# Layer-norm sums: VectorE adds the eight feature tiles, one tensor product sums over the partitions

## The reference

```python
def layer_norm(x, g, b):
    xf = x.astype(jnp.float32)
    mu = jnp.mean(xf, -1, keepdims=True)
    var = jnp.mean(jnp.square(xf - mu), -1, keepdims=True)
    return ((xf - mu) * lax.rsqrt(var + LN_EPS) * g + b).astype(x.dtype)

h = x * (1 + mod[:, 1]) + mod[:, 0]
x = layer_norm(ALPHA * x + 0.5 * mod[:, 2] * swiglu(h, ...), ln_g[l, 0], ln_b[l, 0])
h = x * (1 + mod[:, 4]) + mod[:, 3]
out, k_a, v_a, k_b, v_b = mixer(l, h)          # one input projection, attention, one output projection
x = layer_norm(ALPHA * x + mod[:, 5] * out, ln_g[l, 1], ln_b[l, 1])
h = x * (1 + mod[:, 7]) + mod[:, 6]
x = layer_norm(ALPHA * x + 0.5 * mod[:, 8] * swiglu(h, ...), ln_g[l, 2], ln_b[l, 2])
```

## Time and profile before

| | us |
|---|---|
| median of 3 runs | 2637.7 |
| lowest and highest run | 2637.45, 2644.15 |
| span of the profiled execution | 2637.8 |
| TensorE busy | 2413.0 (91%) |
| VectorE busy | 894.8 (34%) |
| the two kinds of sums (L504), busy: of `Y`, of `SQ` | 43.0, 53.4 |

### The profile page before, as it was taken

One profiled execution on the slowest core, in us unless ns is written; L12 is line 12 of the kernel. 1 busy time (PEld: TensorE's weight loads), 2 busy tenths in 40 slices (PEclk: granted clock), 3 DMA queues, 4 the chain that ended last, 5 costly groups with the idle time before them and its releaser, 6 DMA issues. The chain is left out here.

```text
span 2637.8 us, 37358 instructions
## 1 busy us (share of the span) xinstructions
PE 2413.0 (91%) x14418; PEld 2238.3 (85%) x14418; DVE 894.8 (34%) x2053; ACT 539.3 (20%) x781; POOL 810.4 (31%) x536
## 2 busy tenths in 40 slices
PE   7899999999999969995898677796999999999996
PEld 4799999999999959983587666785999999999995
DVE  0422221122222390006266766138322222222225
ACT  2211111111111121211133223213111111111114
POOL 2522222322233142223365433433333233222310
PEclk9899999999999989995899888897999999999998
DMA  9532323123111001116810000120111111111101
GB/s 307 185 96 80 95 80 95 55 73 95 32 48 40 17 8 48 48 56 174 203 38 30 17 25 17 35 71 14 48 48 48 48 43 43 41 48 48 40 1 64
DMA packets 211414, 171.56 MB, mean 65 GB/s; under 512 B 31848, under 2 KB 191704, under 8 KB 210841
## 3 DMA queue, kind: packets, MB, share of 16 engines
q1 hardware_dynamic: 211352, 170.76, 21.7%
HBM read 157.24 MB, written 19.26 MB: 67 GB/s over the span
## 5 line engine op out<-in xcount | busy, mean ns | idle before, releaser
L193 PE MATMUL psum<-Hhi,Whi 128*128 128x344 f32 x2736 | 880.9, 322 | 46.0 <-POOL Hlo L660 26.4
L195 PE MATMUL psum<-Hhi,Wlo 128*128 128x344 f32 x2736 | 877.9, 321 | 0.0
L194 PE MATMUL psum<-Hlo,Whi 128*128 128x344 f32 x2736 | 877.5, 321 | 0.0
L289 POOL TENSOR_TENSOR Wlo<-RAW,Whi 128x1024 fp32r<-128x1024 f32 x158 | 381.8, 2435 | 688.1 <-ACT Whi L285 687.4
L193 PEld LDWEIGHTS psum<-Hhi,Whi 128*128 128x128 f32 x2736 | 518.4, 189 | 49.9 <-issue 36.1
L195 PEld LDWEIGHTS psum<-Hhi,Wlo 128*128 128x128 f32 x2736 | 518.2, 189 | 0.0
L194 PEld LDWEIGHTS psum<-Hlo,Whi 128*128 128x128 f32 x2736 | 517.6, 189 | 0.2
L376 DVE TENSOR_TENSOR GF<-SIL,psum 128x344 f32<-128x344 f32 x132 | 67.7, 513 | 897.8 <-ACT SIL L358 897.8
L389 DVE SCALAR_TENSOR_TENSOR Y<-psum,G,Y 128x344 f32<-128x344 f32 (+1 forms) x528 | 302.6, 573 | 181.0 <-PE psum L195 181.0
L193 PE MATMUL psum<-Ghi,Whi 128*128 128x344 f32 x1056 | 339.8, 322 | 1.7 <-DVE yS L392 1.7
L194 PE MATMUL psum<-Glo,Whi 128*128 128x344 f32 x1056 | 338.2, 320 | 0.0
(11 more groups left out here) (196 smaller groups left out, 1889.4 us busy)
## 6 DMA issues: line engine op xcount, KB each, us to landing
ADA<-in_w_ada SPq DMA_DIRECT2D x36, 1024.0 KB, 8.5
RAW<-in_ffn_wg SPq DMA_DIRECT2D x44, 512.0 KB, 3.8
RAW<-in_ffn_wu SPq DMA_DIRECT2D x44, 512.0 KB, 3.8
RAW<-in_ffn_wd SPq DMA_DIRECT2D x44, 512.0 KB, 3.3
RAW<-in_w_in SPq DMA_DIRECT2D x18, 512.0 KB, 3.8
bias_rows<-bias_heads SPq DMA_DIRECT2D x4, 1536.0 KB, 15.8
SK<-in_cache_a_k SPq DMA_DIRECT2D x24, 256.0 KB, 3.3
SK<-in_cache_a_v SPq DMA_DIRECT2D x24, 256.0 KB, 4.2
```

The source lines that it names most:

```text
L193: pe.matmul(out, whi, xhi, start=first, stop=False)
L194: pe.matmul(out, whi, xlo, start=False, stop=False)
L195: return pe.matmul(out, wlo, xhi, start=False, stop=last)
L289: pool.tensor_tensor(Wlo[slot][:, :, :], RAW[raw][:, :, :], Whi[slot][:, :, :].bitcast(F32), ALU.subtract).then_inc(W[phase].ready, 1)
```

## The change

`mean_sum` and `var_sum` are new: one VectorE instruction each, a `tensor_reduce` over the view `p k t -> p t k`, adds the eight feature tiles of a group into the new tile `RED[g]` (128 x 344). `mean_pe` and `var_pe` then wait for that and do a single product of `meanw` with `RED[g]`. The order of all three engines is changed with it. New semaphores are `ln_msum` and `ln_vsum`.

```diff
@@ ffn_pe
                 if norm is not None and g:
-
-                    pe.wait_ge(x.y_evac, UNIT_D * (CH - 1) + KT * g + 3)
                     mean_pe(pe, norm, g - 1)
@@ ffn_dve
+                if norm is not None and g < NG - 1:
+                    dve.wait_ge(x.y_evac, UNIT_D * (CH - 1) + KT * (g + 1) + 3)
+                    mean_sum(dve, norm, g)
                 if norm is not None and g == 1:
                     center(dve, norm, 0)
@@
-        def sum_pe(pe, out, src):
-
-            for k in range(KT):
-                last = pe.matmul(out, meanw[:, :], src(k), start=(k == 0), stop=(k == KT - 1))
-            return last
+        def mean_sum(dve, n, g):
+
+            dve.tensor_reduce(RED[g][:, :], Y[:, :, group(g)].rearrange("p k t -> p t k"), AXX,
+                              ALU.add).then_inc(ln_msum, 1)
+
+        def var_sum(dve, n, g):
+            dve.wait_ge(ln_squared, n.n_at(g))
+            dve.tensor_reduce(RED[g][:, :], SQ[:, :, group(g)].rearrange("p k t -> p t k"), AXX,
+                              ALU.add).then_inc(ln_vsum, 1)
 
         def mean_pe(pe, n, g):
-            sum_pe(pe, bank[MEAN_BANK[g]][:, 0:TG], lambda k: Y[:, k, group(g)]).then_inc(ln_mean, 1)
+            pe.wait_ge(ln_msum, n.n_at(g))
+            pe.matmul(bank[MEAN_BANK[g]][:, 0:TG], meanw[:, :], RED[g][:, :], start=True, stop=True).then_inc(ln_mean, 1)
 
         def var_pe(pe, n, g):
-            pe.wait_ge(ln_squared, n.n_at(g))
-            sum_pe(pe, bank[VAR_BANK[g]][:, 0:TG], lambda k: SQ[:, k, group(g)]).then_inc(ln_var, 1)
+            pe.wait_ge(ln_vsum, n.n_at(g))
+            pe.matmul(bank[VAR_BANK[g]][:, 0:TG], meanw[:, :], RED[g][:, :], start=True, stop=True).then_inc(ln_var, 1)
@@ norm_pe
-            var_pe(pe, n, 0)
             mean_pe(pe, n, 2)
-            var_pe(pe, n, 1)
-            var_pe(pe, n, 2)
+            for g in range(NG):
+                var_pe(pe, n, g)
@@ norm_dve
             center(dve, n, 1)
+            var_sum(dve, n, 0)
+            center(dve, n, 2)
+            var_sum(dve, n, 1)
             scaled(dve, n, 0)
-            center(dve, n, 2)
+            var_sum(dve, n, 2)
             scaled(dve, n, 1)
@@ norm_act
             square(act, n, 0)
             square(act, n, 1)
             std(act, n, 0)
-            if n.i == 1:
-                std(act, n, 1)
+            square(act, n, 2)
+            std(act, n, 1)
             input_hi(act, n, 0, 0)
             input_hi(act, n, 0, 1)
-            square(act, n, 2)
-            if n.i != 1:
-                std(act, n, 1)
@@ vector engine, norm 1 (norm 3 likewise)
             samples_in(dve)
             dve.sem_inc(resid_done, 1)
+            mean_sum(dve, ln[1], 2)
             prep(dve, 3, 4, 0)
@@ vector engine, norm 2
             dve.wait_ge(wout_evac, NG * KT + 6)
+            mean_sum(dve, ln[2], 0)
+            mean_sum(dve, ln[2], 1)
             samples_in(dve)
             dve.sem_inc(resid_done, 1)
+            mean_sum(dve, ln[2], 2)
             prep(dve, 6, 7, 1)
```

More of the change, by code:

```diff
@@ L174, in build @@
             RSTD.append(arena.at(f"RSTD{g}", [P, TG], F32, o)); o += up32(4 * TG)
+        RED = []
+        for g in range(NG):
+            RED.append(arena.at(f"RED{g}", [P, TG], F32, o)); o += up32(4 * TG)
         SQ = arena.at("SQ", [P, KT, T], F32, HOFF + 4 * KT * T)
@@ L249, in build @@
         ln_lo, ln_y, ln_small = (sem(x) for x in ("ln_lo", "ln_y", "ln_small"))
+        ln_msum, ln_vsum = sem("ln_msum"), sem("ln_vsum")
         resid_done = sem("resid_done")
@@ L1830, in _ @@
             dve.sem_inc(resid_done, 1)
+            mean_sum(dve, ln[3], 2)
             prep(dve, None, None, 2, last_norm=True)
```

## The result

| | before | after |
|---|---|---|
| median, us | 2638.0 | 2688.7 |
| lowest and highest run | 2637.45, 2644.15 | 2685.52, 2695.99 |
| span of the profiled execution | 2637.8 | 2686.1 |
| TensorE busy | 2413.0 | 2353.4 |
| VectorE busy | 894.8 | 977.6 |

The ratio is 1.019, with a 95% interval of 1.0176 to 1.0205: the changed kernel is slower. The direction was forecast, with 2672 us; the time lies 17 us above that and just above the range, which ended at 2686.

What follows compares the result with a forecast made beforehand. VectorE's chain was taken to bound the norms, though TensorE, 91% busy, mostly sets the end. Last chunks 6.2, clock 5.0, norms 10.4, 6.4 and 5.9 sum to 33.9 us on 2637.8: 2672 us, range 2646 to 2686.

Steps and rivals of the forecast that it cites:

- R: Time of each of 18 added VectorE reductions: taken as 4.3 us, with 3.0 and 4.9 for the range.
- 24-value row: Profile row of a VectorE reduction of 24 jumping values, 180 ns; gave 1.5 ns a value and R = 4.3 us.
- TensorE's 1.7 ns: TensorE's price a column with jumping operands, from eight records of 256 columns in 3.81 us; gave R = 4.9 us.
- costlier jumps: Rival: banks or the long 4128-byte step put R above 4.9, say 5.9 us; 2684 to 2700 us, chance 0.10.
- Last chunks: Last down-product chunks before norms 1 and 3: TensorE waits for evacuations behind reductions, +3.1 us each, +6.2 together.
- clock: Last chunks: after 5.2 us of TensorE idling, the five last units run at half clock for a while; 2.5 us twice, +5.0.
- norm 1: Four reductions on VectorE less 6.8 us of idling filled, no wait left: 4R - 6.8 = +10.4 us.
- norm 3: Four reductions less 10.4 us of idling, +6.8 us; about 0.9 comes back from ScalarE's earlier last root: +5.9.
- norm 2, to the first subtraction: Three reductions ahead of `prep`, which escapes GpSimd's splits: center 0 at 1782.7 in place of 1778.9, +3.8 us.
- norm 2, behind it: Rest of norm 2: three reductions less 10.3 us of VectorE idling filled, 3R - 10.3 = +2.6 us.
- R + 1.3 - 2.8 and R + 4.3 - 8.3: Last chunk: TensorE's wait at group 1's fourth unit, 2.8 us, and added delay to group 2's fourth unit, +0.3.
- 15 us for each us of R: Whole kernel: added time per us of R, 4 in the last chunks and 4, 3 and 4 in the norms.

Runs made afterwards that it cites:

- e7: Changed kernel with 20 and 34 extra unread TensorE products in the two stalls of each last chunk; 2678.3 us, ratio 1.016.
- e9: Changed kernel with norm 2's `samples_in` moved ahead of its reductions of groups 0 and 1; 2685.2 us against 2689.6 for the changed kernel rerun.
- e4: Changed kernel with only the means summed by reductions, the variance sums again eight products each, new order kept; 2659.1 us, ratio 1.0084.
- e1: Changed kernel with each reduction adding eight neighbouring tokens instead of one token's eight tiles, same counts; 2646.6 us, ratio 1.0035.
- e6: Changed kernel plus 13 VectorE reductions and copies at various steps behind the last output copy; 2752 values took 5.04 us at the real step, 3.02 side by side.

## Why the prediction was wrong in size, point by point

**R, the step that failed.** The term that was mis-sized is R, the time of one reduction: 4.3 us in the sum, 5.1 measured (5.06 to 5.34), eighteen times over. The prediction took 1.5 ns a value from the 24-value row: (180 - 144)/24, with a fixed part of 141 to 144 ns. Measured, the rate is 1.79. Only 24 x 1.79 = 43 ns of that row's 180 are rate; with a fixed part of 137 instead of 141 ns it gives 1.79 as well. An error of 4 ns in the fixed part, divided by 24 and multiplied by 2752, is 0.5 us in R. I named the row nearest in kind and moved its fixed part up only, where moving it down gave 5.1 us. The far larger rows were closer: TensorE's 1.7 ns gave 4.9, the upper bound, still 0.2 short of the measured 5.1. Read more closely that row would have given 5.0: its eight records take 0.63 us each and overlap, so they start (3.81 - 0.63)/7 = 0.45 us apart, 1.77 ns a column. The rival "costlier jumps", which held the time that came (2684 to 2700), had its mechanism wrong: the long step adds next to nothing to one of 16 bytes.

**The formulas with the measured R.** Last chunks 2 x 5.0, clock 5.0, norm 1 4 x 5.08 - 6.8 = 13.5, norm 2 5.9 + 4.9 = 10.8, norm 3 9.0: 48.3 us, which is the measured difference of the spans. That it fits to the tenth is luck, as the terms show:

| us | predicted | with the measured R | measured |
|---|---|---|---|
| last chunks, without the clock | 6.2 | 10.0 | 10.3 |
| clock there | 5.0 | 5.0 | 5.0 |
| norm 1 | 10.4 | 13.5 | 12.6 |
| norm 2, to the first subtraction | 3.8 | 5.9 | 9.2 |
| norm 2, behind it | 2.6 | 4.9 | 5.1 |
| norm 3 | 5.9 | 9.0 | 8.6 |
| everything else | 0 | 0 | -2.5 |

The measured parts of the last chunks come from e7: its chunks, at full clock, are 5.7 and 5.6 us longer than before, less 0.5 each for their longer reductions; the clock is what is left of +8.4 and +6.9.

**Last chunks: right.** They were forecast by R + 1.3 - 2.8 and R + 4.3 - 8.3. With 5.24 and 5.34 these make 3.7 and 1.3 us, 5.0 a chunk; the first stall was 3.59. With the 5.5 and 5.59 of e7 they make 4.0 + 1.6 = 5.6, as its chunks have it.

**Clock: right in size, incomplete in place.** It cost 3.2 and 1.8 us, where 2.5 and 2.5 were forecast. It was not foreseen that the clock also falls at the first stall (0.50 from 898), which it did in chunk 1 and not in chunk 2, at equal stalls of 3.59 us. In e9 the same remainder is 5 us in both chunks and in the second of e4 5.4, so 0 to 3.0 a chunk was too narrow a bound. The cost goes with the time at half clock, which the mean clock of a window gives: 0.88 over 29 us is some 7 us and cost 1.8, 0.83 over 30 us is 10 and cost 3.2, 0.79 over 32 us is 13 and cost 5.

**Norm 1: right in mechanism.** No wait is left but one of 0.62 us for the third root. It came 0.9 below the formula, which is mostly scaled 1: 5.00 us before, beside GpSimd, and 3.99 after, since it now falls into a gap of GpSimd's.

**Norm 2: one thing missed.** The prediction asked how `prep` and the reductions stand to GpSimd's splits and was right on both: the reductions kept their time, and `prep`, pushed behind the splits, ran its eight steps in 1.8 us. It gave `samples_in` 0.5 us in the same stretch, though its first operation has two operands in SBUF, and that cost 4.4 us, as e9 shows. Less the 1.2 that `prep` beat its allowance by, 5.9 becomes 9.1. The recorded sum has a slip of 0.2 us here: 12.9 + 0.5 + 3 from 1766.1 is 1782.5, not 1782.7, and the same sum at R = 4.9 gives 9.8 and not the 9.2 of the range's upper bound. Neither changes the outcome.

**Norm 3: right.** 9.0 by the formula, 8.6 measured.

**The slope.** 15 us for each us of R was too flat. In the formulas themselves it is 4 + 4 + 3 + 3 + 4 = 18; I counted norm 2 once, since GpSimd held `prep` at R = 3.0, though above that both its parts grow. Between e1 and the changed kernel the stretches give some 17.

## What to carry to other kernels

Before work is moved from a busy engine to an idle one, ask who waits for whom in that stretch: TensorE was 91% busy in the whole program and yet not the bound in the norms, where seven eighths of its sums had cost nearly nothing, while VectorE's chain set the end. Cost a strided operation by the step of its innermost reads, with a row that is large enough for the rate to outweigh the fixed part; a row of 24 values can't price one of 2752. And look beside each operation that is pushed later at what GpSimd does by then, and whether rows show that kind of operation waiting for it: here additions of two SBUF operands and one-operand TENSOR_SCALARs did, reductions and the subtraction with an operand in PSUM did not.

## What the runs showed of the hardware

- VectorE's reduction costs 1.05 ns a value at steps of 4 and 8 bytes, 1.32 at 12 and 1.7 to 1.8 from 16 bytes to 4128 (e6, with 0.14 us taken as fixed). A copy of 2752 values goes from 1.59 to 2.65 us when its reads jump and to 3.48 when its writes do: the copy pays in another proportion, and more for writes.
- The reductions of the last chunks took 5.24 and 5.34 us where two of the same shape took 5.06, and 5.50 to 5.59 when TensorE was busy beside them all the time. Why is open.
- A two-operand operation of VectorE of 0.23 us waited 4.4 us for GpSimd and, in three traces, was not let in between two of its instructions; in e4 it was, and so were the steps of `prep` in the kernel before, which each waited for one (2.3 us).
- The price of equal stalls of TensorE (3.59 and 6.11 us) at the clock was 1.8 to 5.4 us a chunk, by how long it stood at 1.2 GHz behind them (some 7 to 13 us). What sets the moment at which it falls or rises is open.
